# Half of a depthwise convolution moved from VectorE to TensorE, four taps to a matmul

## The reference, cut to what matters

```python
def conformer_conv_mix(h, w_in, dw_w, dw_b, ln_g, ln_b, w_out):
    a, a_gate, z = jnp.split(h @ w_in, 3, axis=-1)      # 256 x 2048 @ 2048 x 6144
    g = a * jax.nn.sigmoid(a_gate)
    pad = CONV_WIDTH // 2                               # CONV_WIDTH = 31
    y = lax.conv_general_dilated(                       # depthwise: each channel by itself
        g, dw_w[:, None, :].astype(g.dtype), window_strides=(1,),
        padding=[(pad, pad)], dimension_numbers=('NWC', 'WIO', 'NWC'),
        feature_group_count=D_BRANCH) + dw_b
    y = jax.nn.silu(layer_norm(y, ln_g, ln_b))
    return (y * jax.nn.silu(z)) @ w_out
```

## Time and profile before

| | |
|---|---|
| median of 3 runs | 3555.81 us (3555.05 to 3561.99) |
| the profiled execution, its own time | 3562.65 us |
| span of its profile | 3561.0 us |
| mean granted TensorE clock | 0.946 |
| PE, DVE, ACT, POOL busy | 91%, 73%, 38%, 6% |
| stage of `ci`, groups 1 to 10 (2768.06 to 3066.76) | 298.70 us |

### The profile page before, as it was taken

How to read it: one execution, slowest core, us unless ns; L and a number is a source line. 1 busy time by engine, 2 the same in 40 slices (tenths; PEclk the granted TensorE clock), 3 DMA queues, 4 the chain that set the end, 5 groups by cost and what they waited for, 6 DMA issues and landing times.

```text
span 3561.0 us, 59751 instructions
## 1 busy us (share of the span) xinstructions
PE 3242.1 (91%) x24466; PEld 3080.0 (86%) x24466; DVE 2598.2 (73%) x3609; ACT 1351.0 (38%) x1442; POOL 203.5 (6%) x389
## 2 busy tenths in 40 slices
PE   5999788999998789989999999899889888799998
PEld 5999667999997569979998999899579888798998
DVE  6887767888886778876676576565766899766554
ACT  3333344343333343343334333433554222434332
POOL 0000000000000000000110010000000000000000
PEclk9999869999999789989999999899899999999999
DMA  5777405757776027756676676377025444366753
GB/s 201 263 264 254 165 18 177 248 204 262 264 263 238 24 76 256 251 192 233 238 274 215 218 256 247 118 283 261 1 97 210 143 140 143 118 236 215 239 186 130
DMA packets 124953, 696.50 MB, mean 196 GB/s; under 512 B 14136, under 2 KB 14288, under 8 KB 66128
## 3 DMA queue, kind: packets, MB, share of 16 engines
q1 hardware_dynamic: 67392, 484.47, 39.5%
q0 software_dynamic: 55296, 201.35, 16.0%
q10 hardware_dynamic: 2064, 7.78, 0.6%
HBM read 691.43 MB, written 2.10 MB: 195 GB/s over the span
## 4 chain that ended last, share of the span: by engine, by line
PE 71%; DVE 17%; ACT 5%; issue 3%; DMA 3%; ACTq 0%; DVEq 0%; POOLq 0%
PE bank L464 19%; PE bank L465 19%; PE bank L466 19%; DVE wlo L1396 4%; DVE yc L1995 4%; DMA aslab<-w_ada_dram 3%; ACT whi L961 2%; PE bank L567 2%; DVE acc L1422 2%; PE bank L558 2%; DVE sc L1555 1%; PE bank L799 1%; PE bank L778 1%; PE bank L502 1%; DVE ulo L1548 1%
## 5 line engine op out<-in xcount | busy, mean ns | idle before, releaser
L464 PE MATMUL bank<-uhi,whi 128*128 128x256 f32 x6784 | 1961.5, 289 | 176.6 <-DVE wlo L1396 83.5
L465 PE MATMUL bank<-ulo,whi 128*128 128x256 f32 x6784 | 1944.0, 287 | 0.0
L466 PE MATMUL bank<-uhi,wlo 128*128 128x256 f32 x6784 | 1943.0, 286 | 0.0
L961 ACT CAST whi<-raw 128x2048 fp32r<-128x2048 f32 (+1 forms) x464 | 875.8, 1889 | 1786.7 <-PE bank L466 1710.1
L1396 DVE TENSOR_TENSOR wlo<-raw,whi 128x2048 fp32r<-128x2048 f32 (+1 forms) x464 | 1053.4, 2272 | 643.0 <-ACT whi L961 642.7
L464 PEld LDWEIGHTS bank<-uhi,whi 128*128 128x128 f32 x6784 | 1327.8, 196 | 193.0 <-issue 124.1
L465 PEld LDWEIGHTS bank<-ulo,whi 128*128 128x128 f32 x6784 | 1327.9, 196 | 0.9
L466 PEld LDWEIGHTS bank<-uhi,wlo 128*128 128x128 f32 x6784 | 1327.0, 196 | 0.0
L1422 DVE SCALAR_TENSOR_TENSOR acc<-aslab,sm,acc 128x512 f32<-128x512 f32 x1008 | 695.5, 745 | 66.0 <-DMA aslab<-w_ada_dram 65.7
L438 POOL DMA_DIRECT2D aslab<-w_ada_dram x384 | 203.1, 529 | 3192.6 <-DVE acc L1422 2484.0
L1995 DVE SCALAR_TENSOR_TENSOR yc<-gp,cols,yc 128x256 f32<-128x256 f32 x480 | 192.9, 476 | 0.0
(11 more groups left out here) (248 smaller groups left out, 2318.0 us busy)
## 6 DMA issues: line engine op xcount, KB each, us to landing
aslab<-w_ada_dram POOLq DMA_DIRECT2D x384, 512.0 KB, 5.5
raw<-w_win_dram SPq DMA_DIRECT2D x96, 1024.0 KB, 5.0
raw<-w_wfi_dram SPq DMA_DIRECT2D x96, 1024.0 KB, 5.4
raw<-w_wfo_dram SPq DMA_DIRECT2D x48, 1024.0 KB, 5.1
raw<-w_wci_dram SPq DMA_DIRECT2D x48, 1024.0 KB, 4.9
raw<-w_wo_dram SPq DMA_DIRECT2D x32, 1024.0 KB, 4.9
raw<-w_wpg_dram SPq DMA_DIRECT2D x32, 1024.0 KB, 5.1
raw<-w_wqz_dram SPq DMA_DIRECT2D x32, 1024.0 KB, 5.1
```

Source lines behind the costliest of these rows:

```text
L464: nc.tensor.matmul(o, whi_, xhi_, start=start, stop=False, skip_group_check=True)
L465: nc.tensor.matmul(o, whi_, xlo_, start=False, stop=False, skip_group_check=True)
L466: return nc.tensor.matmul(o, wlo_, xhi_, start=False, stop=stop, skip_group_check=True)
L961: nc.scalar.copy(whi[:, s % 2, 0:n], raw[:, s, 0:n]).then_inc(s_hi, 1)
```

## The change

DVE keeps the pairs of blocks 0-1, 4-5, 8-9, 12-13; the blocks 2, 3, 6, 7, 10, 11, 14, 15 (`PE_BLOCKS`) go to TensorE. For one of them, four copies of `gp`'s block, each of 32 channels and shifted by 0, 1, 2, 3 tokens, are stacked on the 128 partitions, once for each quarter c of the 128 channels (`shifted`, 4 x 284 columns). The host makes the matching weights `wcv`: 128 x 32 matrices that are diagonal in each of the four stacked parts. A matmul of such a matrix by 256 columns adds four taps for 32 channels, and its result goes to 32 partitions of a PSUM bank; 8 steps q x 4 quarters c = 32 float32 matmuls do the 31 taps of one block (`conv_block`). They come behind slabs 1 and 3 of groups 3, 5, 7 and 9. POOL issues for each block one load of the weights (512 KB) and 16 copies within SBUF (32 partitions x 284 numbers each). ACT adds the bias and moves the result to `yc` (`conv_copy`). DVE's steps between splits go from 17, 17, 17 to 10, 9, 9. The loop over the groups of `ci` in PE's program is written out. Nothing outside this layer's code changes.

```diff
--- before.py
+++ after.py
@@ -242,7 +242,7 @@
         kc = tiles(sb("kc", 4 * T, at=arena + 36864))
         vx = tiles(sb("vx", 2 * T, at=arena + 40960))
         vc = tiles(sb("vc", 2 * T, at=arena + 43008))
-        PADT = T + 30
+        PADT = T + 32
         gp_t = sb("gp", KT * PADT, at=arena)
         gp = gp_t[:, :].rearrange("p (k n) -> p k n", n=PADT)
         zs_t = sb("zs", KT * T, at=arena + KT * PADT * 4)
@@ -250,6 +250,10 @@
         yc_t = sb("yc", KT * T, at=arena + KT * PADT * 4 + 16384)
         yc = tiles(yc_t)
         k2 = sb("k2", K2_N, at=arena + 52224)
+        SHIFT = T + 28
+        shifted = [k2[:, K2_AX:K2_AX + 4 * SHIFT], zs_t[:, 2048:2048 + 4 * SHIFT]]
+        taps = [pt[:, :], sc[:, 0:1024]]
+        assert K2_AX + 4 * SHIFT <= K2_N and KT * PADT * 4 + 2 * 16384 <= 52224
         assert arena + 52224 + K2_N * 4 <= 229368 and base <= 229368, (base, arena)
         dft = k2[:, K2_DFT:K2_DFT + 1024].rearrange("p (k n) -> p k n", k=2)
         chan = k2[:, K2_CHAN:K2_CHAN + 512].rearrange("p (k n) -> p k n", k=2)
@@ -328,6 +332,9 @@
         s_f2 = sem("dft_even_odd_ready")
         s_fe = sem("dft_even_copied")
         s_fb = sem("dft_combined")
+        s_cl_ = [sem(f"conv_shifts_and_taps_loaded{i}") for i in range(2)]
+        s_cp = sem("conv_block_multiplied")
+        s_cc = sem("conv_block_copied")
         s_cg = sem("conv_gates_ready")
         s_conv = sem("conv_done")
         s_lnq = sem("conv_squares_ready")
@@ -361,6 +368,8 @@
 
             return [h // 8 for h in gate_halves(r, q - 3) if h % 8 == 7] if q >= 3 else []
 
+        PE_BLOCKS = [4 * (i // 2) + 2 + i % 2 for i in range(8)]
+
         def conv_squares(c):
             return (sq[:, 0:1024], sq[:, 1024:2048], pt[:, :], sq[:, 0:1024])[c]
 
@@ -446,7 +455,20 @@
             with pool.Fori(1, ADA_BOTH) as a:
                 group(a, True)
             group(ADA_BOTH, False)
-            with pool.Fori(ADA_BOTH + 1, ADA_GROUPS) as a:
+            with pool.Fori(ADA_BOTH + 1, RUN["co"]["a0"]) as a:
+                group(a, False)
+
+            pool.wait_ge(s_nl, 16 * (U_NORMS["nci"] + 1))
+            for i, b in enumerate(PE_BLOCKS):
+                if i >= 2:
+                    pool.wait_ge(s_cp, i - 1)
+                pool.dma_start(taps[i % 2], w["wcv"][i]).then_inc(s_cl_[i % 2], 16)
+                pool.wait_ge(s_drain, 2 * (RUN["ci"]["e0"] + b // 2 + 1))
+                for j in range(4):
+                    for c in range(4):
+                        pool.dma_start(shifted[i % 2][32 * j:32 * j + 32, SHIFT * c:SHIFT * (c + 1)],
+                                       gp[32 * c:32 * c + 32, b, j:j + SHIFT]).then_inc(s_cl_[i % 2], 16)
+            with pool.Fori(RUN["co"]["a0"], ADA_GROUPS) as a:
                 group(a, False)
 
 
@@ -877,16 +899,37 @@
             project("ao", "ya")
 
             norm("nci")
-            project("ci", "nci", n=10)
-            project("ci", None, g0=10, n=1)
+            r = RUN["ci"]
+
+            def conv_block(i):
+
+                pe.wait_ge(s_cl_[i % 2], 16 * 17 * (i // 2 + 1))
+                if i >= 2:
+                    pe.wait_ge(s_cc, i - 1)
+                for q in range(8):
+                    for c in range(4):
+                        at = 32 * (4 * q + c)
+                        last = nc.tensor.matmul(bank[6 + i % 2][32 * c:32 * c + 32, 0:T],
+                                                taps[i % 2][:, at:at + 32],
+                                                shifted[i % 2][:, SHIFT * c + 4 * q:SHIFT * c + 4 * q + T],
+                                                start=q == 0, stop=q == 7, skip_group_check=True)
+                last.then_inc(s_cp, 1)
+
+            def behind(g, s):
+                if g in (3, 5, 7, 9) and s % 2:
+                    conv_block(g - 3 + s // 2)
+            for g in range(11):
+                group(r, g, (r["e0"] + g) % 2, slab_t, "nci" if g == 0 else None,
+                      lambda s, g=g: behind(g, s))
 
             for c in range(4):
-                pe.wait_ge(s_conv, 4 * c + 4)
+                pe.wait_ge(s_conv, 2 * c + 2)
+                pe.wait_ge(s_cc, 2 * c + 2)
                 for k in range(4):
                     last = nc.tensor.matmul(bank[5][:, 0:T], ones[:, :], yc[:, 4 * c + k, :],
                                             start=c == 0 and k == 0, stop=c == 3 and k == 3)
             last.then_inc(s_lns, 1)
-            project("ci", None, g0=11, n=1)
+            group(r, 11, (r["e0"] + 11) % 2, slab_t)
 
             for c in range(4):
                 pe.wait_ge(s_lnq, c + 1)
@@ -1341,6 +1384,8 @@
                     if g == 8:
 
                         act.wait_ge(s_drain, 2 * (r["e0"] + 8))
+                    if g == 10:
+                        act.wait_ge(s_cp, 8)
                     for half in range(2):
                         at = 1024 * (g - 8) + 512 * half
                         last = nc.scalar.activation(zs_t[:, at:at + 512], bank[2 * par + half][:, :],
@@ -1348,12 +1393,21 @@
                     last.then_inc(s_drain, 2)
             split(r, 0, 2)
             split(r, 0, 3)
+            def conv_copy(i):
+                act.wait_ge(s_cp, i + 1)
+                b = PE_BLOCKS[i]
+                nc.scalar.activation(yc[:, b, :], bank[6 + i % 2][:, 0:T], ACT.Identity,
+                                     bias=col("conv_dw_b_2", b)).then_inc(s_cc, 1)
             for g in range(1, 12):
                 split(r, g, 0)
                 split(r, g, 1)
+                if g in (4, 6, 8, 10):
+                    conv_copy(g - 3)
                 drain_ci(r, g - 1, (r["e0"] + g - 1) % 2)
                 split(r, g, 2)
                 split(r, g, 3)
+                if g in (3, 5, 7, 9):
+                    conv_copy(g - 3)
             for c in range(4):
                 act.wait_ge(s_lnr, c + 1)
                 if c == 3:
@@ -1970,7 +2024,7 @@
 
             def conv_steps():
 
-                for k in range(0, KT, 2):
+                for k in range(0, KT, 4):
                     for t in range(TAPS):
                         for b in (k, k + 1):
                             x = gp[:, b, t:t + T]
@@ -2014,11 +2068,11 @@
                 split(r, g, 1)
                 if g <= 8:
                     drain_ci(g - 1)
-                conv_some(17)
+                conv_some(10)
                 split(r, g, 2)
-                conv_some(17)
+                conv_some(9)
                 split(r, g, 3)
-                conv_some(17)
+                conv_some(9)
             dve.wait_ge(s_lns, 1)
             mu = sc[:, 512:768]
             link(v.tensor_scalar(mu, bank[5][:, 0:T], 1.0 / D, None, ALU.mult))
@@ -2131,6 +2185,15 @@
     out["wao"] = slabs_of(a["attn_w_out_2"][0], full)
     ci = [c for g in range(8) for c in (256 * g, 256 * g + P, D + 256 * g, D + 256 * g + P)]
     out["wci"] = slabs_of(a["conv_w_in_2"][0], ci + run_of(2 * D, 16))
+    dw = np.asarray(a["conv_dw_w_2"][0])
+    taps = np.zeros((8, P, 8, 4, 32), dw.dtype)
+    lane = np.arange(32)
+    for i in range(8):
+        b = 4 * (i // 2) + 2 + i % 2
+        for t in range(dw.shape[0]):
+            for c in range(4):
+                taps[i, 32 * (t % 4) + lane, t // 4, c, lane] = dw[t, P * b + 32 * c + lane]
+    out["wcv"] = taps.reshape(8, P, 1024)
     out["wco"] = slabs_of(a["conv_w_out_2"][0], full)
     return out
```

## The result

The changed kernel takes 3513.75 us (median of 4 runs, 3512.45 to 3517.68) against 3558.9 us (4 runs, 3555.05 to 3565.35): ratio 0.9868, 95% interval 0.9847 to 0.9889. Two more series on other occasions gave 0.9877 (0.9858 to 0.9896) and 0.9884 (0.9865 to 0.9902), in medians 41.7 and 41.9 us. The forecast was 37.0 us, a ratio of 0.9896: the direction, and eight to nine tenths of the size. On the forecast's scale the first ratio gives 0.9868 x 3555.81 = 3509 us, 3 us under the low end of the range. The two later ratios give 3512 and 3515 us, just inside it.

What follows compares the result with a forecast made beforehand. VectorE was taken to bound groups 1 to 10, TensorE next. TensorE's slabs 230.4, blocks 29.3 and misses 2 gave 261.7 us against 298.7, so 3555.81 - 37.0 = 3518.8, say 3519 us; range 3512 to 3547.

Steps and rivals of the forecast that it cites:

- The bound, and what frees it: Groups 1 to 10 of `ci`: VectorE bounds at 298.7 us; after removing 248 steps TensorE's 230.4 us does, worth at most 68.3.
- The block: TensorE's 32 narrow float32 matmuls per convolution block: 3.5 us, plus 0.1 at each change of weights; eight blocks 29.3 us.
- case of 4.4 us a block: TensorE's convolution blocks: at the skill page's efficiency, 0.79 of the ideal, 4.4 us each, the stage 7 us longer.
- two at a time: Rival, chance 0.11: TensorE overlaps only pairs of column tiles; a block costs 6.9 us, gain 11 us, whole 3545.
- queueing in one tile: Rival, chance 0.05: the four column tiles queue on TensorE; a block costs 13.8 us, +44 us, whole 3600.
- the turning point at 8.5 us a block: Convolution blocks on TensorE: block cost at which gain turns to loss, (298.7 - 230.4)/8, an overlap of 1.6.
- The stage: Groups 1 to 10 of `ci`: 230.4 + 29.3 + 2 = 261.7 us against 298.7, a gain of 37.0 us.
- missed splits: VectorE's splits coming late for TensorE's slabs: 2 us over the stage, below it nothing, above it about 8.
- a change of form: TensorE switching between full and narrow weights around blocks: 0.1 us at each of 16 changes, 1.6 us in all.
- the 2 to 5 us a group that were expected: Sign of the forecast: VectorE idle some 2 to 5 us in each group, waiting for `whi`.
- Transfers, ScalarE: POOL's 17 issues a block at 0.53 us, landing 5.5 us later; ScalarE's eight `conv_copy` of about 0.5 us: nothing on the path.
- the step that takes everything outside the stage as unchanged: Outside groups 1 to 10: the 52.7 us tail to `co` keeps its instructions; the written-out loop is taken at nothing.

## Why the prediction was nearly right, and where it fell short

**The bound, and what frees it.** As predicted: VectorE's period went, TensorE's 5.76 us a slab took its place, the waits for `wlo` went from 45.3 us to none and the clock to 1.00.

**The block.** Predicted 3.5 + 0.2 us, measured 3.78: four tiles at once. The prediction's case of 4.4 us a block, overlap at 0.79 of the ideal, did not come: a step of four tiles costs 0.432 us, as much as one wide matmul, so all of the ideal was reached. The order of issue is what the gain hangs on. The price of the rival "two at a time" is shown at 6.4 us a block and 16 us of gain in place of 42; that of queueing in one tile at 11.6 us and a loss of 24, so the turning point at 8.5 us a block lies between the two, as worked out.

**The stage.** Predicted 261.7 us, measured 260.64; two terms were off, 2 us for missed splits (nothing) and 0.1 us for a change of form (0.16, 0.9 us more over the stage), and what is left of them is the 1.1 us. VectorE waits more for `whi` than the 2 to 5 us a group that were expected, 66.7 us over ten groups, at no cost.

**Transfers, ScalarE.** As predicted: 0.50 us an issue against 0.53 assumed, landings of 4.8 us, 7.0 at worst, none waited for by TensorE. The eight copies of the sums wait 13.3 us in all for TensorE, on no path.

**What failed** is the step that takes everything outside the stage as unchanged; the sum has no term for it. The reason given was for one part of it: "The written-out loop changes only how instructions are fetched; I take it at nothing". Kernels with a written-out loop and nothing else were 0.13 to 0.17% faster, about 5 us by the ratios and 2.3 to 6.7 in medians; by what mechanism stays open. For the other part, `co`, none was given. The tail up to `co` is what it was, 52.7 us, but `co` starts better. Its first slab, before (first line) and after:

```profile
3119.47:3127.91 8.44, 8.44 (x48) 0.65 0.01 2
```
```profile
3073.37:3080.49 7.12, 7.12 (x49) 0.79 0.01 2
```

More of it ran at full clock, 1.3 us, and 1.7 us are gone by the end, in all three profiles of the changed kernel (439.7 to 439.9 us from `co` to the end against 441.5). But the change does not bring this by itself. In the run with tiles in pairs, which has every other part of the change, the same stretch of `co` has the clock of before, and `co` to the end takes 442.3 us; in the run with one tile after the other it takes 441.2:

```profile
3094.25:3102.69 8.44, 8.44 (x49) 0.65 0.01 2
```

The kernel before with the added array, whose program is unchanged, took 440.7. The clock rises at different points of the first slabs, and what sets the point isn't shown.

The stage's 38.1 and these 1.7 us are 39.8; the 2 us that are left to the 41.7 and 41.9 of the two later series are about the least that a written-out loop brought by itself. The first series' 45 to 47 us has chance in it, and it is by this chance as much as by the step that failed that its ratio falls outside the range, which the two later ones do not. The range was too narrow at its low end all the same: 3512 lies 7 us under the forecast, of which 4 were for the sum (no misses and exact overlap, 3515). That left 3 us for all that lies outside the stage and for the choice of executions, while the runs of the kernel before spread by up to 21 us within a series.

## What to carry to other kernels

Before moving work off an engine that paces a stage, write down the next engine's floor, here 40 slabs of 5.76 us, and what the move adds to it; the gain is the distance to that floor, not the 98 us taken off. Here narrow matmuls paid only when they were issued by turns over the tiles: the same 32 instructions cost 3.8, 6.4 or 11.6 us by their order alone. When the receiving engine has become the bound, look at once for idle time on the first: giving two blocks back shortened the stage by another 7.6 us.

## What the runs showed that I had not expected

TensorE overlaps column tiles in the order in which the matmuls are issued: four by turns 3.78 us a block, two by turns 6.4, one after the other 11.6, all at a granted clock of 1.00. Where one tile follows the other, it starts the next tile's work beside the last two matmuls of the tile before, four records, and no earlier. A step of four narrow float32 matmuls of 256 columns costs 0.432 us, exactly one wide one. An issue on POOL costs 0.50 us for 8 partitions as for 32, and 0.53 for 128 partitions of 4 KB: at these sizes POOL's time goes by the number of copies, hardly by their size.
